# Sample state updates in stacked rows, and the rotation of queries and keys on VectorE

## The reference, cut to what matters

```
q = rotate(q, pos); k = rotate(k, pos) * RET_K_DIM ** -0.5
scores = (q @ k.T) * decay
o      = scores @ v + (q @ s_prev) * exp(log_g * (idx + 1))
k_dec  = k * exp(log_g * (c - 1 - idx))
s_new  = exp(log_g * c) * s_prev + k_dec.T @ v
rotate: x1 * cos - x2 * sin | x1 * sin + x2 * cos   (halves of the 256)
```

## Time and profile before

| | |
|---|---|
| time, median of 3 runs | 3501.99 us (3501.92 to 3509.51) |
| the profiled execution's own time | 3502.55 us |
| its span in the profile | 3500.8 us |
| retention with its tiles (`layer_one`) | about 2682 us to the end |
| busy in the span | PE 95%, DVE 61%, ACT 32%, POOL 6% |
| mean granted TensorE clock | 0.99 of full speed |

### The profile page before, as it was taken

One profiled execution on the slowest core, in us unless ns is written; L12 is line 12 of the kernel. 1 busy time (PEld: TensorE's weight loads), 2 busy tenths in 40 slices (PEclk: granted clock), 3 DMA queues, 4 the chain that ended last, 5 costly groups with the idle time before them and its releaser, 6 DMA issues.

```text
span 3500.8 us, 65609 instructions
## 1 busy us (share of the span) xinstructions
PE 3339.9 (95%) x25476; PEld 2967.5 (85%) x25476; DVE 2123.7 (61%) x3225; ACT 1118.6 (32%) x1646; POOL 200.8 (6%) x157
## 2 busy tenths in 40 slices
PE   7998999999999999888999999999999999999997
PEld 7987888788788878678999999999999777777787
DVE  5466565656666666336666666766665345666655
ACT  4222232222222232214433333333332343223223
POOL 1000000000000000002000000000000222222200
PEclk9999999999999999899999999999999999999999
DMA  5466888788888888753533333333335565555534
GB/s 182 148 202 212 280 281 279 249 275 286 263 267 278 280 268 279 236 186 134 161 105 119 117 124 100 124 124 117 118 106 173 195 218 201 201 196 196 196 128 157
DMA packets 477799, 679.33 MB, mean 194 GB/s; under 512 B 32561, under 2 KB 283570, under 8 KB 474354
## 3 DMA queue, kind: packets, MB, share of 16 engines
q1 hardware_dynamic: 434882, 618.88, 53.5%
q10 hardware_dynamic: 42192, 55.98, 4.5%
q0 software_dynamic: 416, 0.28, 0.1%
HBM read 583.92 MB, written 89.52 MB: 192 GB/s over the span
## 4 chain that ended last, share of the span: by engine, by line
PE 83%; DVE 8%; issue 3%; DMA 2%; ACT 1%; SPq 1%; POOL 0%; DVEq 0%; ACTq 0%; POOLq 0%
PE low_banks L1270 56%; PE high_banks L1270 25%; PE high_banks L1273 3%; DVE WL L1902 2%; DMA area<-in_cache_v 1%; DVE area L2003 1%; SPq L1158 1%; DVE area L1988 1%; DVE area L2265 0%; ACT WH L1585 0%; DVE XL L2346 0%; DVE area L2013 0%; DMA area<-in_cache_k 0%; DMA WR<-in_w_in_ret 0%; DVE area L1976 0%
## 5 line engine op out<-in xcount | busy, mean ns | idle before, releaser
L1270 PE MATMUL low_banks<-XH,WH 128*128 128x288 f32 (+2 forms) x4632 | 1126.4, 310 | 36.0 <-DVE WL L1902 11.6
L1270 PE MATMUL low_banks<-XH,WL 128*128 128x288 f32 (+2 forms) x4632 | 1062.8, 297 | 0.0
L1270 PE MATMUL low_banks<-XL,WH 128*128 128x288 f32 (+2 forms) x4632 | 1060.9, 296 | 0.0
L1270 PEld LDWEIGHTS low_banks<-XH,WH 128*128 128x128 f32 x4632 | 769.3, 190 | 171.9 <-issue 139.5
L1270 PEld LDWEIGHTS low_banks<-XL,WH 128*128 128x128 f32 x4632 | 772.5, 190 | 0.0
L1270 PEld LDWEIGHTS low_banks<-XH,WL 128*128 128x128 f32 x4632 | 771.6, 189 | 0.0
L1270 PE MATMUL high_banks<-area 128*32 128x256 f32 (+7 forms) x4912 | 610.9, 456 | 34.8 <-DMA area<-in_cache_v 16.2
L1270 PEld LDWEIGHTS high_banks<-area 128*32 128x32 f32 (+3 forms) x4912 | 274.0, 139 | 244.8 <-issue 177.3
L1585 ACT ACTIVATE WH<-WR 128x1024 fp32r<-128x1024 f32 x272 | 287.4, 1057 | 545.5 <-PE low_banks L1270 453.6
L1902 DVE TENSOR_TENSOR WL<-WR,WH 128x1024 fp32r<-128x1024 f32 x272 | 343.7, 1264 | 131.2 <-ACT WH L1585 125.6
L2003 DVE STREAM_TRANSPOSE area<-area 128x512 f32<-128x512 f32 x512 | 335.1, 691 | 111.5 <-PE high_banks L1270 59.3
(11 more groups left out here) (184 smaller groups left out, 3260.7 us busy)
## 6 DMA issues: line engine op xcount, KB each, us to landing
area<-in_cache_k SPq DMA_DIRECT2D x512, 256.0 KB, 4.8
area<-in_cache_v SPq DMA_DIRECT2D x512, 256.0 KB, 5.3
area<-in_w_in_ret SPq DMA_DIRECT2D x162, 512.0 KB, 5.7
WR<-in_w_in_attn SPq DMA_DIRECT2D x136, 512.0 KB, 5.4
WR<-in_w_out_ret SPq DMA_DIRECT2D x66, 512.0 KB, 3.8
area<-in_state_ret SPq DMA_DIRECT2D x64, 512.0 KB, 7.5
out<-area SPq DMA_DIRECT2D x64, 512.0 KB, 5.4
WR<-in_w_in_ret SPq DMA_DIRECT2D x38, 512.0 KB, 4.0
```

Source lines behind the costliest of these rows:

```text
L1270: return nc.tensor.matmul(out, a, b, start=start, stop=stop, skip_group_check=True)
```

## The change

It has four parts.

1. The sample state update becomes a float32r product. The three terms (high x high, low x high, high x low) are stacked as rows: of each 32 rows, 8 hold one sequence's keys and values as term one, 8 as term two, 8 as term three, and 8 are zero. So one float32r product of 32 rows takes the place of one float32 product of 32 rows. The number of products stays four for each `rs_state`.
2. The stacked rows are made in another way. `load_v3` (slot 20) fetches the values from DRAM, each row to three places and a fourth that is cleared later, in eight DMAs of 32 rows; `store_k` (slot 26) writes `kn_s` to DRAM, and `load_k3` (slot 29) fetches it back in eight DMAs after that write has landed. `pad_v` (slot 32) and `pad_k` (slot 36) are two ACT copies and one DVE operation each. `pad_rows`, `rs_mask` and two memsets of `pads` go.
3. `rope` of heads 1 to 7 moves from POOL to DVE, at slots 3 and 12.
4. `rs_state` moves to slots 39, 48, 57 and 65, and the samples' gate to slot 71. In slots 39, 48 and 57 `rs_state` of chunk c is put in the list before `ret_scores` of chunk c + 1, which stands in the same slot.

```diff
-        put(-13 + which, Stage("rope", which=which, early=h == 0))
+        put(-13 + (9 if h else 1) * which, Stage("rope", which=which, early=True))
     put(9, Stage("rs_keys"))
-    put(10, Stage("pad_rows"))
-    put(17, Stage("rs_mask"))
+    put(4, Stage("load_v3"))
+    put(10, Stage("store_k"))
+    put(13, Stage("load_k3"))
+    put(16, Stage("pad_v"))
+    put(20, Stage("pad_k"))
...
-        put(24 + 9 * c - (c == 3), Stage("rs_state", g_=c // 2, e=c % 2))
+        put(23 + 9 * c - (c == 3), Stage("rs_state", g_=c // 2, e=c % 2))
...
-    put(51, Stage("gate", t=4, norm=norms[4]))
+    put(55, Stage("gate", t=4, norm=norms[4]))
...
+            def thrice(to, rows):
+                per = rows.rearrange("(j g i) n -> j g i n", g=2, i=NQ)
+                for j, n in itertools.product(range(4), range(2)):
+                    yield to[32 * j:32 * j + 32, n, :], per[j, n].rearrange("(o i) n -> o i n", o=1).broadcast_to([4, NQ, rows.shape[1]])
+
+            def load_v3(g):
+                for n in ("full6", "full7", "rvn_in"):
+                    sp.wait_ge(sem[n], c.before(n))
+                for to, rows in thrice(v3, values_d[SEQ:T, 512 * g:512 * g + 512]):
+                    sp.dma_start(to, rows).then_inc(sem["v3_in"], 16)
+
+            def store_k(g):
                 sp.wait_ge(sem["drained5"], c.before("drained5"))
+                sp.wait_ge(sem["k3_in"], c.before("k3_in"))
+                sp.dma_start(keys_d, kn_s[:]).then_inc(sem["k_out"], 16)
+
+            def load_k3(g):
+                sp.wait_ge(sem["k_out"], c.before("k_out"))
                 sp.wait_ge(sem["kz_ready"], c.before("kz_ready"))
+                for to, rows in thrice(k3, keys_d):
+                    sp.dma_start(to, rows).then_inc(sem["k3_in"], 16)
...
                 for j in range(4):
                     rows = slice(32 * j, 32 * j + 32)
-                    mm(bank[4 + j][:, :], kz[rows, g_, e * 128:(e + 1) * 128], rvz[rows, :]).then_inc(sem[f"full{4 + j}"], 1)
+                    mm(bank[4 + j][:, :], kz[rows, g_, e * 128:(e + 1) * 128], vz[rows, g_, :]).then_inc(sem[f"full{4 + j}"], 1)
...
+            def pad_v(g):                       # ACT
+                act.wait_ge(sem["v3_in"], c.before("v3_in"))
+                act.wait_ge(sem["head_in"], c.before("head_in"))
+                for n in range(4, 8):
+                    act.wait_ge(sem[f"full{n}"], c.before(f"full{n}"))
+                copy(vz, v3)
+                copy(v3, v3, scale=hc[:, 387:388]).then_inc(sem["pad_hi"], 1)
+
+            def pad_k(g):
+                act.wait_ge(sem["k3_in"], c.before("k3_in"))
+                copy(kz, k3, scale=hc[:, 384:385])
+                copy(k3, k3, scale=hc[:, 385:386]).then_inc(sem["pad_hi"], 1)
...
+            def pad_v(g):                       # DVE
+                dve.wait_ge(sem["pad_hi"], c.done("pad_hi"))
+                v.scalar_tensor_tensor(out=vz, in0=vz.bitcast(f32), scalar=hc[:, 388:389], in1=v3, op0=MUL, op1=ADD).then_inc(sem["kz_ready"], 1)
+
+            def pad_k(g):
+                dve.wait_ge(sem["pad_hi"], c.done("pad_hi"))
+                v.scalar_tensor_tensor(out=kz, in0=kz.bitcast(f32), scalar=hc[:, 386:387], in1=k3, op0=MUL, op1=ADD).then_inc(sem["kz_ready"], 1)
```

More of the change, by code:

```diff
@@ L169, in adds @@
         "rs_keys": {"full4": 1, "full5": 1, "drained4": 1, "drained5": 1, "qd_ready": 1},
-        "pad_rows": {"padded_in": 128}, "rs_mask": {"kz_ready": 1},
+        "load_v3": {"v3_in": 128}, "store_k": {"k_out": 16}, "load_k3": {"k3_in": 128},
+        "pad_v": {"pad_hi": 1, "kz_ready": 1}, "pad_k": {"pad_hi": 1, "kz_ready": 1},
         "ret_scores": {"full4": 1, "full5": 1, "drained4": 1, "drained5": 1},
@@ L986, in hybrid_step_kernel @@
         used[0] = after_inputs
-        rvz = lay("rvz", [128, 512])
+        rounded = mixes.rearrange("p a k n -> p (a k n)")
+        kz, vz = [rounded[:, at:at + 2 * n].rearrange("p (g n) -> p g n", g=2) for at, n in ((kz_at, 256), (vz_at, 512))]
+        v3 = oN[:, 2:4, :]
         rst, decay8 = lay("rst", [128, 10]), lay("decay8_sb", [128, HEADS])
@@ L1256, in _ @@
                                   load_x_tile=load_x_tile, load_norm=load_norm, load_pages=load_pages, load_rope=load_rope, load_tables=load_tables,
-                                  load_quads=load_quads, store_state=store_state, load_qk=load_qk, load_rvn=load_rvn, load_g4=load_g4, pad_rows=pad_rows, pads=pads))
+                                  load_quads=load_quads, store_state=store_state, load_qk=load_qk, load_rvn=load_rvn, load_g4=load_g4, load_v3=load_v3, store_k=store_k, load_k3=load_k3, pads=pads))
         @block.tensor
@@ L1857, in _ @@
                                 ret_scores=lambda g, c: ret_scores(g, c), ret_out=lambda g, c: ret_out(g, c),
-                                rs_keys=rs_keys, rs_out=rs_out, store_state_p=store_state_p, split_g=split_g,
+                                rs_keys=rs_keys, rs_out=rs_out, store_state_p=store_state_p, split_g=split_g, pad_v=pad_v, pad_k=pad_k,
                                 y_sq=y_sq, x_sq=x_sq, x_scale=x_scale, x_tr=x_tr, store_x=store_x, quad_split=quad_split,
@@ L2248, in ret_state @@
                     if c_:
-                        ins = v.scalar_tensor_tensor(out=Sp[:, e, :], in0=Sp[:, e, :], scalar=hc[:, 387:388], in1=bank[4 + e][:, :],
+                        ins = v.scalar_tensor_tensor(out=Sp[:, e, :], in0=Sp[:, e, :], scalar=hc[:, 390:391], in1=bank[4 + e][:, :],
                                                      op0=MUL, op1=ADD)
@@ L2355, in _ @@
                                 ret_scores=lambda g, c: ret_scores(g, c), ret_state=lambda g, c: ret_state(g, c),
-                                ret_rstd=ret_rstd, rs_keys=rs_keys, rs_mask=rs_mask, rs_state=rs_state, gate=gate))
+                                ret_rstd=ret_rstd, rs_keys=rs_keys, pad_v=pad_v, pad_k=pad_k, rs_state=rs_state, gate=gate))
         @block.gpsimd
```

45 lines of the change are left out of this document (15 added, 30 removed).

## The result

The changed kernel takes 3556.5 us (median of 4 runs, 3547.5 to 3566.6), the kernel before beside it 3502.2 (3501.9 to 3509.5): 1.015 of the time, 95% interval 1.0132 to 1.0167. It is 54.3 us slower. The forecast was 3537 with a range up to 3550: the sign was right, the size 20 us short. It is also the one with the lowest mean granted clock: 0.980, where the other three have 0.985, 0.985 and 0.986.

A forecast was written before the change was run, and what follows sets the result against it. PE, busy 95%, was taken as the bound, gaining only if DVE keeps up. Terms 15.7 + 16.7 - 0.3 - 3 - 2.1 + 7.5 gave +34.5 us on 3502.55: 3537, range 3510 to 3550.

The forecast's parts named there:

- The three places of part 4: Slots 39, 48, 57: `ret_scores` directly behind `rs_state` waits for DVE's drains; +15.7 us, bounds -19 and +20.
- The joins: Joins into heads 3 to 7: PE waits 4.1 and 1.9 us for additions behind DVE's rotations; +16.7 us.
- Head 1's wait for L2306: Join into head 1, `turn_v` needing bank 6: waits of 1.3 and 4.2 become about 0.75 and 2.7; -3 us.
- The product: Each of 32 `rs_state` stages: four float32r products take 0.35 us, saving PE 0.8, bounds 0.2 to 0.9.
- The clock: Behind the five joins' 4.1 us waits TensorE runs at the lower clock for a while; +7.5 us, bounds 0 and +10.
- Part 2, costed at nothing: Making the stacked rows: keys' round trip covered by `rs_out`, ACT at 32%; no cost, bound +1 a head, +8.
- rival d: The keys' round trip through DRAM is late, on top of the forecast: 3545 us; chance 0.1.
- (a): PE's saving counts and the waits do not come: about -43, with ropes partly covered -30, 3472 us; chance 0.13.
- (b): Slots 39 to 57 hide their drains (-19) while the join is as computed: 0, 3502 us; chance 0.07.
- (c): Waits as computed but the clock stays up: 3529 us, within the forecast's range; forecast with this together 0.7.

The follow-up runs named there:

- changed, keys at once: Changed kernel with the samples' keys' copies reading rows of the values, so not waiting for the keys' write: 3546.5 us, 1.012 of the kernel before.
- rotation back on POOL: Changed kernel with the rotation of heads 1 to 7 back on POOL at its old slots: 3533.4 us, 1.0077 of the kernel before.
- old slots: Changed kernel with `rs_state` back at its old slots, one tile behind `ret_scores` of the next chunk: 3522.1 us, 1.0048 of the kernel before.
- stack only: Changed kernel with the rotation back on POOL and `rs_state` at its old slots, samples' gate still at slot 71: 3493.1 us, 0.9967 of the kernel before.
- stack, float32 product: Stacked rows, gate at slot 71, rotation on POOL, `rs_state` at old slots, but rows multiplied as float32, not float32r: 3517.3 us, 1.0056 of the kernel before.
- order alone: Kernel before with only `rs_state` moved to slots 39, 48, 57, 65, ahead of `ret_scores` of the next chunk: 3518.3 us, 1.0043.
- rotation on DVE alone: Kernel before with only the rotation of heads 1 to 7 moved to DVE at slots 3 and 12: 3538.3 us, 1.0096.
- gate later: Kernel before with only the samples' gate moved from slot 67 to slot 71: 3497.5 us, 0.9982.

## Why the prediction fell short

**A ledger.** If waits, product and clock are all there is, the span should change by the change of PE's idle time, less 32 x 0.64 = 20.5 us where the short product is in, plus half of the added time at the lower clock (from 2680 us to the end; before: 32.2 idle, 23.3 low, span 3500.8):

| kernel | PE idle | low clock | worked out | measured (span) |
|---|---|---|---|---|
| changed | 87.0 | 77.9 | +61.6 | +64.0 |
| changed, keys at once | 84.3 | 40.8 | +40.4 | +45.9 |
| rotation back on POOL | 61.8 | 68.4 | +31.7 | +33.4 |
| old slots | 63.2 | 58.3 | +28.0 | +27.1 |
| stack only | 36.8 | 26.9 | -14.1 | -12.2 |
| stack, float32 product | 37.4 | 36.7 | +11.9 | +11.4 |
| order alone | 46.4 | 15.8 | +10.5 | +15.1 |
| rotation on DVE alone | 57.8 | 37.3 | +32.6 | +35.8 |
| gate later | 28.4 | 28.6 | -1.2 | -1.1 |

It closes within 5.5 us in every kernel, so in the profiled executions nothing large is hidden outside these three. By it the steps stand so:

- **The three places of part 4** (+15.7): right. 29.0 us of waits less 24 x 0.64 saved is +13.6.
- **The joins** (+16.7, waits of 4.1 and 1.9): right in place and size (3.96 and 1.70; ten waits, 28.3 us, for 30 forecast). `rs_keys` follow each other at 94 to 96 us from head 3 on, where 91 was forecast; the rest is the two points below. Head 1's wait for L2306 was 2.6 for 2.7 forecast.
- **The product** (0.8 each): 0.64. Over 32 stages that is 5 us.
- **The clock** (+7.5, bounds 0 and +10): right for the join, where it was applied: with the keys at once it comes to (40.8 - 23.3) / 2 = 8.8 us. In the profiled execution of the changed kernel it is 27.3, since the prediction gave the waits of `ret_scores` no part in it. In the other three it must be less: a mean clock higher by 0.005 to 0.006 is, over some 3550 us, 35 to 43 us less at half rate (an estimate). The Trainium skill (TensorE: Matmul & The Clock Gate, Part 1) has an idle TensorE gated to 1.2 GHz; the rows agree as to direction (0.50 after the idle of 3.96), but idle of 1.44 us was followed by 0.50 in one kernel and by 1.00 in the other.
- **Part 2, costed at nothing** (bound +8, rival d): this is the step that failed. "Landed after some 3 to 5 us" was 8.2. "Is needed at 3065.5, when `rs_out` ends" left out that ACT's other work for PE, emptying bank 6, stands behind `pad_k`. "SP is held at `store_k` and `load_k3`, with weights two steps ahead behind it: nothing" left out the states' loads, which stand among the new transfers. Part 2 costs 20 us by itself (float32 product against gate later; spans of the profiled executions 12.5, of which 9 are waits and 4 the clock's). In the changed kernel the wait for the keys alone costs 10 by the medians and 18 in the profiled executions; there the ledger puts 2.7 down to waits and 18.5 to the clock, with the doubt about that execution told above.

One slip in the prediction's working: 25 x 0.80 + 0.35 + 5 x 0.44 is 22.55, not 22.4, which would add 0.75 us over five joins.

By single edits on the medians: gate -5, making of the rows +20, product -24, rotation +29, order with the short product on top +34: 54. These steps form one chain from the kernel before to the changed one, so that they add up is no check. The 34.5 forecast and the 20 of part 2 make 54.5; that this agrees so closely is luck, with the product's 5 us missed. What the values' and states' lateness cost apart from the keys' stays open, since every edit that helped one delayed another; so does why the lower clock came after some short waits and not after others. With the keys at once 9.5 us over the forecast remain, of which the product explains 5.

**The rivals.** (a), faster, came true for one part only: the product's saving counts if nothing behind it waits for DVE. (b), hidden drains, is refuted by the 24 waits. (c), no clock, by the windows. (d), late keys, was true on top of the forecast, at 0.1 chance and with too small a price.

**What beats both kernels** is stack only: 3493.1 us, 0.9967 of before (0.9956 to 0.9979), 63 us less than the changed kernel. Its lead over the later gate alone (3497.5) is within the noise: the product gives 24 us and the making of its rows takes 20 of them back. The moves of the rotation and of `rs_state` are what costs most.

## What to carry to other kernels

Lay out the neighbour engine's queue by hand around a move, with each operation's length: 9 us of rotation a head cost 23 to 34 us in lumps and 5 us in pieces. A consumer put directly behind its producer turned part of the producer's saving into a wait. A profile is one execution: compare its mean clock with the other runs' before a sum over its low stretches is put down to the edit. And a transfer "hidden" behind an engine at 32% must be followed to what stands behind it on that engine, with the landing time of a queue that is already loaded, before it is costed at nothing.

## What the runs showed of the hardware

- The granted clock fell to 0.50 for stretches of about 3.4 us after waits of only 1.4 to 1.7 us (changed kernel, heads 2 to 7), and stayed at 1.00 after the same waits within the heads in the kernel with the keys at once.
- The 64 KB write of the keys landed 5.1 to 8.2 us after its issue by SP among the states' loads (changed kernel), and 2.7 us (median) after a later issue by POOL (stack only).
- The subtraction that makes `WL` took 1.22 us alone and up to 3.26 while POOL rotated.
- Four float32r products of 32 rows and 512 columns, in four groups of rows, take 0.50 us together, eight float32 records of that shape 1.14.
